# A mixture-of-experts stage recast: 32-token groups on four column tiles in fp32, 20 ring places, results added on the chip

## What is computed

```
def moe_swiglu(h, w_router, b_router, w_gate, w_up, w_down):
    ht = h.reshape(B * S, D)                        # 256 x 1024
    logits = (ht @ w_router).astype(jnp.float32) + b_router.astype(jnp.float32)
    top_v, top_i = lax.top_k(logits, TOP_K)         # 2 of 8
    probs = jax.nn.softmax(top_v, axis=-1)
    gates = jnp.sum(jax.nn.one_hot(top_i, N_EXPERTS, dtype=jnp.float32) * probs[..., None], axis=1)
    out = jnp.zeros((B * S, D), jnp.float32)
    for e in range(N_EXPERTS):                      # D_FF_EXPERT = 3584
        a = jax.nn.silu(ht @ w_gate[e]) * (ht @ w_up[e])
        out = out + gates[:, e:e + 1] * (a @ w_down[e]).astype(jnp.float32)
    return out.astype(h.dtype).reshape(B, S, D)
```

## Time and profile before

| | |
|---|---|
| time, median of 3 runs | 1631.44 us (1629.76 to 1632.03) |
| span of the profiled execution | 1628.0 us; the median of the runs is 3.4 us above it |
| PE busy | 1576.8 us (97%) |
| DVE, ACT, POOL busy | 981.2, 764.3, 91.4 us |
| mean granted TensorE clock | 0.995 of full |
| DMA | 498.81 MB, mean 306 GB/s |
| expert stage: item 0 on PE from | 773.3 us |
| last matmul of the last item's last slot starts | in the group at 1618.86 us |

### The profile page before, as it was taken

One profiled execution on the slowest core, in us unless ns is written; L12 is line 12 of the kernel. 1 busy time (PEld: TensorE's weight loads), 2 busy tenths in 40 slices (PEclk: granted clock), 3 DMA queues, 4 the chain that ended last, 5 costly groups with the idle time before them and its releaser, 6 DMA issues.

```text
span 1628.0 us, 19519 instructions
## 1 busy us (share of the span) xinstructions
PE 1576.8 (97%) x7744; PEld 1167.7 (72%) x7744; DVE 981.2 (60%) x918; ACT 764.3 (47%) x747; POOL 91.4 (6%) x169
## 2 busy tenths in 40 slices
PE   9999999999999999999998999889998799999997
PEld 8888888888898888888346884358852488888632
DVE  6877478555568875586017980059830388888411
ACT  4455574443343536663017760047720377777400
POOL 1021000000000030000220000000000000000000
PEclk9999999999999999999999999999999999999999
DMA  8666256656445552478999999999999999999998
GB/s 293 224 207 207 78 207 220 222 182 202 124 162 182 205 176 73 134 258 325 403 392 418 417 419 417 417 418 418 419 418 417 419 418 418 417 418 392 367 420 331
DMA packets 156214, 498.81 MB, mean 306 GB/s; under 512 B 8412, under 2 KB 13284, under 8 KB 141604
## 3 DMA queue, kind: packets, MB, share of 16 engines
q1 hardware_dynamic: 152608, 483.44, 77.2%
q0 software_dynamic: 3520, 14.18, 2.3%
HBM read 492.59 MB, written 8.40 MB: 308 GB/s over the span
## 4 chain that ended last, share of the span: by engine, by line
PE 85%; DMA 10%; ACT 2%; DVE 1%; SPq 1%; issue 0%; DVEq 0%; ACTq 0%
PE ps L976 23%; PE ps L977 23%; PE ps L978 23%; PE ps L981 14%; DMA sb_const<-in_moe_w_gate_dram 4%; PE ps L985 3%; DMA sb_z<-in_moe_w_gate_dram 3%; DMA sb_raw_w<-in_moe_w_down_dram 1%; DMA sb_z<-in_moe_w_down_dram 1%; SPq L660 1%; DMA sb_ringa<-in_w_in_dram 1%; ACT sb_w L1723 0%; DVE sb_low_masks L504 0%; ACT sb_whi L498 0%; DVE sb_wlo L443 0%
## 5 line engine op out<-in xcount | busy, mean ns | idle before, releaser
L976 PE MATMUL ps<-sb_whi,sb_hhi 128*128 128x512 f32 (+2 forms) x1304 | 510.4, 391 | 15.0 <-DVE sb_low_masks L504 14.5
L978 PE MATMUL ps<-sb_wlo,sb_hhi 128*128 128x512 f32 (+2 forms) x984 | 377.1, 383 | 0.0
L977 PE MATMUL ps<-sb_whi,sb_hlo 128*128 128x512 f32 (+2 forms) x856 | 326.9, 382 | 0.0
L976 PEld LDWEIGHTS ps<-sb_whi,sb_hhi 128*128 128x128 f32 x1304 | 246.8, 189 | 68.7 <-issue 19.8
L978 PEld LDWEIGHTS ps<-sb_wlo,sb_hhi 128*128 128x128 f32 x984 | 184.9, 188 | 36.4
L504 DVE TENSOR_TENSOR sb_low_z<-sb_z,sb_whi 128x2048 fp32r<-128x2048 f32 x84 | 191.5, 2290 | 30.1 <-ACT sb_whi L498 30.1
L443 DVE TENSOR_TENSOR sb_wlo<-sb_z,sb_whi 128x2048 fp32r<-128x2048 f32 (+1 forms) x68 | 148.8, 2195 | 73.9 <-ACT sb_whi L428 73.8
L498 ACT ACTIVATE sb_whi<-sb_z 128x2048 fp32r<-128x2048 f32 x84 | 161.5, 1924 | 61.1 <-PE ps L978 45.9
L977 PEld LDWEIGHTS ps<-sb_whi,sb_hlo 128*128 128x128 f32 x856 | 161.1, 188 | 29.4
L428 ACT ACTIVATE sb_whi<-sb_z 128x2048 fp32r<-128x2048 f32 (+1 forms) x68 | 125.4, 1846 | 116.0 <-PE ps L978 115.0
L977 PE MATMUL ps<-sb_whi,sb_hhi 128*128 128x512 f32 x448 | 178.4, 398 | 0.0
(11 more groups left out here) (373 smaller groups left out, 2047.1 us busy)
## 6 DMA issues: line engine op xcount, KB each, us to landing
sb_z<-in_moe_w_gate_dram SPq DMA_DIRECT2D x56, 1024.0 KB, 21.1
sb_z<-in_moe_w_up_dram SPq DMA_DIRECT2D x56, 1024.0 KB, 17.0
sb_z<-in_moe_w_down_dram SPq DMA_DIRECT2D x56, 1024.0 KB, 18.6
sb_ringa<-in_w_in_dram SPq DMA_DIRECT2D x43, 1024.0 KB, 5.0
sb_raw_wlo<-in_moe_w_gate_dram SPq DMA_DIRECT2D x32, 1024.0 KB, 14.9
sb_z<-in_w_in_dram SPq DMA_DIRECT2D x24, 1024.0 KB, 5.2
sb_raw_wlo<-in_moe_w_down_dram SPq DMA_DIRECT2D x24, 1024.0 KB, 14.9
sb_ringa<-in_moe_w_gate_dram SPq DMA_DIRECT2D x16, 1024.0 KB, 19.9
```

What stands on the lines that cost most here:

```text
L976: nc.tensor.matmul(out, lh, rh, start=start, stop=False)
L977: nc.tensor.matmul(out, ll, rh, start=False, stop=False)
L978: return nc.tensor.matmul(out, lh, rl, start=False, stop=stop)
```

## The change

The expert stage is rewritten; mixer and dense part stay. In the words of the code:

- **No split.** `whi4`, `wlo4`, `low_*`, `e_hi_of`, `e_lo_of` and the two-part tokens and activations are gone. All items multiply in fp32 from the landed slot.
- **Groups of 32 tokens (`QC`) on four column tiles.** A small item has two groups (64 tokens), a large one three: `CAP` becomes 96. For each k tile and group, four matmuls take the same 32 tokens in the four column tiles, each with a quarter of the columns. In down, two groups and two halves of the output columns fill the four tiles; the third group of a large item fills them with two k rows and two halves.
- **Slots.** 46 an item: gate and up hold one k tile each, of 2048 columns (step 0) or 1536 (step 1), down two rows a partition. 20 ring places, the six new ones over `whi`, `hhi`, `ahi`/`alo` and `ringa0` among others; the router's split weights move to `rows`.
- **Early slots.** Slots 0 to 2 of item 0 are issued ahead of w_out (after `dsc_sb` and `do_out`), slot 3 among the w_out loads, 4 and 5 after `y_half`, 6 and 7 after `yt_turned`, the next as places of w_out come free.
- **Results added on the chip.** `out_rows`, its stores and the last gathers are gone. In the next item's first gate product, after k = 1 and k = 4, `scatter` multiplies `pick_t` (one-hot, times the gate) by `ysb`, and DVE adds the banks to x (`add_rows`). `pick_places` makes `pick_t` from rows that `spread_rows_all` spread once. In item 0, ACT's `y_out` waits for `last_ok`.
- **Extra items** may now belong to any expert, twice to one of over 192 tokens.
- SP's loop waits with a lag read from `eid`, since the ring's places shift by item; the last item has its own constants (`LAST_PLACE`).

```diff
-EXTRA = TT * S // P
+EXTRA = 5
...
+QC = P // 4
+CAP = 3 * QC
+E_SLOTS = 46
+PLACES = 20
+S_G, S_U, S_D = (0, 16), (8, 28), (24, 36, 40)
+E_WIDE = (4 * C, FE - 4 * C)
+LAST_PLACE = (7 * E_SLOTS) % PLACES
...
+        half_z = [z[:, t, c:c + SLOT] for c in (Z_DQ + S, Z_G + 2 * C, Z_MV, 0) for t in range(TT)]
+        out_lanes = [(1 * (A_SLOTS + F_SLOTS) + S_TAIL + 6 + n) % RING_L for n in range(3)]
+        place = [const[:, at_decay:at_decay + SLOT], *half_z[0:2], raw_heads[:, :], *half_z[2:], ringa1[:, :], ringa0[:, :],
+                 *(w[:, k, :] for k in out_lanes for w in (raw_whi, raw_wlo)), raw_hlo[:, :], raw_hhi[:, :]]
...
+            if rows_in(s) == 2 and s < S_D[2]:
+                d = s - S_D[0] if s < S_U[1] else s - S_D[1] + 4
+                return wd[bass.ds(e * FE + d * (2 * P), 2 * P), :].rearrange("(p k) n -> p k n", k=2)
+            if rows_in(s) == 2:
+                q, r = (s - S_D[2]) // 3, (s - S_D[2]) % 3
+                f0, n = SLOT + 2 * q * BLK, BLK
+                if r < 2:
+                    return wd[bass.ds(e * FE + f0 + r * n, n), :].rearrange("(p b) n -> p b n", b=3)[:, 0:2, :]
+                return wd[bass.ds(e * FE + f0, 2 * n), :].rearrange("(c p b) n -> p c b n", c=2, b=3)[:, :, 2, :]
+            step = 0 if s < S_G[1] else 1
+            m = 0 if s in range(S_G[step], S_G[step] + KD) else 1
+            k = s - (S_G, S_U)[m][step]
+            return gu[m][bass.ds(e * D + k * P, P), step * SLOT:step * SLOT + E_WIDE[step]].unsqueeze(1)
...
+                if layer > 0:
+                    sp.wait_ge(dsc_sb, 2 * NG * DEPTH)
+                    into(0, 0, 0)
+                    sp.wait_ge(do_out, DEPTH)
+                    for s in (1, 2):
+                        into(0, s, 0)
                 for s in range(4):
                     load(layer, "A", S_BR + 5 + s, part(a["w_out"][layer], KH * (s % 2), KH, s // 2 * C, C))
+                    if layer > 0 and s == 1:
+                        wait_used(sp, 1, "A", S_BR + 1)
+                        into(0, 3, 0)
...
+                    def load_in_loop(j):
+                        e = expert(j)
+                        lag = sp.value_load(eid[0:1, bass.ds(j + 16, 1)], min_val=0, max_val=E_SLOTS - 32)
+                        for s in range(E_SLOTS):
+                            if s < E_SLOTS - 2 * PLACES:
+                                sp.wait_ge(eaten, (j - 1) * E_SLOTS + lag + (E_SLOTS + s + 1 - PLACES))
                             else:
+                                wait_eaten(sp, j, s - PLACES)
+                            into(j, s, e)
...
+                    for s in range(4, E_SLOTS):
+                        if s == 4:
+                            sp.wait_ge(y_half, 4 * DEPTH)
+                        elif s == 6:
+                            sp.wait_ge(yt_turned, 4 * DEPTH)
+                        elif s in (8, 10, 11):
+                            wait_lo(sp, 1, "A", S_BR + 6 + (8, 10, 11).index(s))
+                        elif s in (12, 14, 16):
+                            wait_used(sp, 1, "A", S_BR + 6 + (12, 14, 16).index(s))
+                        elif s == 18:
                             sp.wait_ge(router_mm, 1)
+                        elif s == 19:
+                            sp.wait_ge(gather_pair, 1)
                         elif s >= PLACES:
+                            wait_eaten(sp, 0, s - PLACES)
+                        into(0, s, 0)
...
+                def e_product(j, s0, step, bank, n_groups, final, after=None):
+                    n = E_WIDE[step] // 4
+                    for k in range(KD):
+                        if first_item(j) and s0 == 0 and k % 2 == 0:
+                            pe.wait_ge((gt_hi, gt_lo)[k // KH], k % KH // 2 + 1)
+                        pe.wait_ge(*signal_of(j, s0 + k, final))
+                        w = slot_of(j, s0 + k, final)
+                        for g in range(n_groups):
+                            for c in range(4):
+                                m = mm(ps[c * QC:(c + 1) * QC, bank + g, 0:n], tok_x[:, k, g * QC:(g + 1) * QC],
+                                       w[:, c * n:(c + 1) * n], k == 0, k == KD - 1)
+                        m.then_inc(eaten, 1)
+                        if after is not None:
+                            after(k)
...
+                def e_down(j, s, n_groups, final):
+                    pe.wait_ge(*signal_of(j, s, final))
+                    w = slot_of(j, s, final).rearrange("p (k n) -> p k n", k=2)
+                    for kk in range(2):
+                        if s < S_D[2]:
+                            d = s - S_D[0] if s < S_U[1] else s - S_D[1] + 4
+                            chunk_, b = d // 2, d % 2 * 2 + kk
+                        else:
+                            q, r = (s - S_D[2]) // 3, (s - S_D[2]) % 3
+                            chunk_, b = (2 * q + r, kk) if r < 2 else (2 * q + kk, 2)
+                        tokens = slice(chunk_ * QC, (chunk_ + 1) * QC)
+                        first, last = s == S_D[0] and kk == 0, s == E_SLOTS - 1 and kk == 1
+                        for h in range(2):
+                            for g in range(2):
+                                at = h * HC + g * QC
+                                m = mm(ps[at:at + QC, 6, :], act_t[:, g, b, tokens], w[:, kk, h * C:(h + 1) * C],
+                                       first, last)
+                        if n_groups > 2:
+                            if kk == 0:
+                                held = b, tokens
+                            else:
+                                for h in range(2):
+                                    for part, (b_, tokens_) in enumerate((held, (b, tokens))):
+                                        at = h * HC + part * QC
+                                        m = mm(ps[at:at + QC, 7, :], act_t[:, 2, b_, tokens_],
+                                               w[:, part, h * C:(h + 1) * C], s == S_D[0], s == E_SLOTS - 1)
+                    m.then_inc(eaten, 1)
...
+                def scatter(j, t, sets, banks):
+                    for h in range(2):
+                        rows_h = slice(h * HC, (h + 1) * HC)
+                        for c in range(sets):
+                            m = mm(ps[:, banks[h], :], pick_t[rows_h, c, t * P:(t + 1) * P], ysb[rows_h, c, :],
+                                   c == 0, c == sets - 1)
+                    return m
+                def scatter_before(j, sets):
+                    def after(k):
+                        if k == 1:
+                            pe.wait_ge(y_ok, j)
+                            pe.wait_ge(pick_step, j * 3)
+                            scatter(j - 1, 0, sets, (3, 4)).then_inc(scat_mm, 1)
+                        elif k == 4:
+                            pe.wait_ge(row_sum, (j - 1) * 2 + 1)
+                            scatter(j - 1, 1, sets, (3, 4)).then_inc(scat_mm, 1)
+                    return after
...
+                def item(j, n_groups, sets_before, next_rows, final=False):
+                    if not first_item(j):
+                        pe.wait_ge(gt_hi, j * 2 + 2)
+                        pe.wait_ge(gt_lo, j * 2 + 2)
+                        pe.wait_ge(e_silu, j * 2)
+                    e_product(j, S_G[0], 0, 0, n_groups, final, None if first_item(j) else scatter_before(j, sets_before))
+                    if first_item(j):
+                        pe.wait_ge(rank_ok, 1)
+                    else:
+                        pe.wait_ge(row_sum, j * 2)
+                    e_product(j, S_U[0], 0, 3, n_groups, final)
+                    pe.wait_ge(e_silu, j * 2 + 1)
+                    def after(k):
+                        if k == 3:
+                            e_turn(j, 0, n_groups)
+                    e_product(j, S_G[1], 1, 0, n_groups, final, after)
+                    copied_back(j, 0)
+                    if not first_item(j):
+                        pe.wait_ge(y_ok, j)
+                    for s in range(S_D[0], S_U[1]):
+                        e_down(j, s, n_groups, final)
+                    e_product(j, S_U[1], 1, 3, n_groups, final)
+                    for s in range(S_D[1], S_D[2]):
+                        e_down(j, s, n_groups, final)
+                    e_turn(j, 1, n_groups)
                     if first_item(j):
                         gather(1, CAP)
+                    elif not final:
+                        turn_gathered(j + 1, next_rows)
+                    copied_back(j, 1)
+                    for s in range(S_D[2], E_SLOTS):
+                        e_down(j, s, n_groups, final)
...
+                def y_out(j, n_groups):
+                    wait_eaten(act, j, E_SLOTS - 1)
+                    nc.scalar.activation(ysb[:, 0:n_groups - 1, :], ps[:, 6:5 + n_groups, :], ACT.Copy).then_inc(y_ok, 1)
...
+                def item(j, n_groups, next_rows):
+                    silu_of(j, 0, n_groups)
+                    copy_first(j, 0, n_groups)
```

(36 more changed lines are left out.)

807 lines of the change are left out of this document (210 added, 597 removed).

## The result

| | before | after |
|---|---|---|
| time, median | 1631.7 us (1629.8 to 1632.0, 4 runs) | 1607.4 us (1607.3 to 1607.6, 4 runs) |
| ratio, 95% interval | | 0.9858 (0.9845 to 0.9872) |
| span of the profiled execution | 1628.0 us | 1605.1 us |
| last slot's matmuls start | 1618.86 us | 1596.14 us |

The kernel is 24.3 us faster. The forecast was 1590, a change of 41 from the 1631.4 it started from: direction and range held, the size did not. The last slot was to land at 1579.2 us and lands at 1596.1; the tail behind it is 9.0 us, forecast 9.3. So the 17 us that are missing all lie ahead of the last landing.

A forecast was written before the change was run, and what follows sets the result against it. The DMA stream of expert weights was taken as the bound; four terms summed to 39.5 us off the 1628.0 us span, giving 1588.5. Adding 3.4 for the median gave 1592, counting upward 1588; forecast 1590, range 1578 to 1614.

The forecast's parts named there:

- The bound: Expert stage: one DMA stream, ending about 9 us before the kernel does, sets the time before and after.
- Term 1: End of the mixer: three more 1 MiB slots fit into idle DMA time, -7.5 us (bounds 0 and -7.5).
- Term 2: Expert stage: 6.0 MB less traffic from result stores, final gathers and smaller token gathers, -14.5 us.
- Term 3: Stretches of the expert stream below 418 GB/s: 20 places and no final gathers recover 8.5 us (bounds 5 and 11).
- Term 4: Gate and up slots: reading 8 or 6 KB runs instead of 4 KB gives -9 us, 13 at most.
- Rival B: Expert stream: longer runs gain nothing, since the place may set the pace; 1599 us, chance 0.15.
- The sum: Whole kernel: the four terms together save 39.5 us, the last slot landing at 1579.2 us.
- PE under the stream: Expert stage: PE needs 114.4 us a large item and 79 a small one; DMA still sets the end, by 5 us.

The follow-up runs named there:

- ring14: Kernel after with the same 20 places, but from slot 20 on each slot waits until the slot 14 before it is used: 1615.2 us, ratio 0.9907.
- before_aligned: Kernel before with its tiles reordered so that all 14 ring places, not 7, begin on an assumed 256-byte boundary: 1623.2 us, ratio 0.9949.

## Why the size was off

- **The bound** was right. One stream of transfers sets the end before and after, and the tail is 9.0 us.
- **The stream's end** has no term in the prediction, which counts bytes at a rate up to the last landing. The sixteen parts of the last slot lag by 6.9 us in the mean, against 1.1 before: 5.8 of the 17 us, by estimate. The deeper ring has a hand in it, since it removes the wait that had drawn the parts together; ring14 shows 5.5 instead of 6.9.
- **Term 1, early slots:** 7.5 forecast, 7.7 measured by undoing it. Whatever they cost the w_out loads is inside this; item 0 begins on PE at 772.2 us, before at 773.3, so it is little. The reason given, a DMA idle over half of 704 to 738 us, misreads the row: its share is 0.56, so 0.44 is idle, 15 us, which still holds three slots.
- **Term 2, results on the chip:** the stores and final gathers were worth 12.5 us, 12.0 by their bytes. The step that failed is the token gathers. I counted 1.0 MB less as 2.5 us gained, and set aside as "only helps" what a gather of few rows costs besides its bytes. In fact the smaller gathers cost 4.1 us. 14.5 forecast, 12.5 - 4.1 = 8.4 found.
- **Term 3, stream below 418:** undoing the early slots and the ring together costs 12.0, so 4.3 of term 3 is the ring. Most of its use is to hold the head start, which the prediction didn't see: with slots from 20 on held to 14 ahead, term 1 would have given 1619.4 - 1615.2 = 4.2 instead of 7.7. The table's writes still dip (364 GB/s from 788 to 804 us), as forecast.
- **Term 4, longer runs:** this is the term that failed in kind. Of "z, eight places of the 20, starts from a faster pace" the first half is true and the second false. I took the pace as a property of the tile z; it goes by the place's first byte, and only three of the eight places in z lie on the boundary. The change made the runs longer and moved the ring from half its places on the boundary to 3 of 20. Undisturbed the stream gained 418 to 419 GB/s, 2 us, for 9 forecast. The two effects are there one by one: long runs +10 to +15 us when taken away, and 12 places on the boundary -11.4. By that price the seven places that would have kept the share at half are 7 x 11.4 / 12 = 6.7 us, an estimate that with the 2 us makes up the 9; as before_aligned gave half of its forecast and the last five places next to nothing, the price per place isn't firm. Rival B had the right outcome for the term, not for its reason.
- **The sum:** 24.3 found. 12.0 (early slots and ring) + 8.4 + 3.9 left for term 4 and the rest of term 3, by subtraction. Against 39.5, short by 4.0, 6.1 and 5.1 us; runs that undo one part each need not add up exactly. The uneven end isn't one more item beside these: it is inside them, since every run has it but the kernel before and before_aligned.
- **PE under the stream:** right, to 0.3 us an item with hardly any DMA beside it and to 1.2 us in a large item with the whole stream beside it (115.6 for 114.4).

Open: why the sixteen parts of a slot drift apart, and what the kernel would gain if they didn't; why the last five places gave so little; why the kernel before gained half of what its places promised; and how a gather of 64 or 96 rows slows the packets.
